# Moving the last chunk of a gated branch's output projection behind the second chunk's state products

## The reference

```python
z, xbc, dt_raw, u, v, ga, gb = split_cols(h @ W['w_in'][l], IN_SIZES)
ya, hs, cs = ssd_branch(z, xbc, dt_raw, conv0[l], ssm0[l], ...)
yb, vr = chunk_mlp_branch(jax.nn.gelu(u), jax.nn.gelu(v), ...)
merged = jax.nn.sigmoid(ga) * (ya @ W['w_ssd_out'][l]) + jax.nn.sigmoid(gb) * (yb @ W['w_cmlp_out'][l])
x = x + g1 * rmsnorm(merged @ W['w_o'][l], W['mix_post_g'][l])
```

```python
def step(h, inp):
    cb = jnp.einsum('btgn,bsgn->btsg', cc, bc)
    mix = cb[..., None] * decay * dtc[:, None]
    y_in = jnp.einsum('btsgr,bsgrp->btgrp', mix, xc)
    y_st = jnp.einsum('btgn,bgrpn->btgrp', cc, h) * jnp.exp(cum)[..., None]
    ...
    h_new = h * jnp.exp(last)[..., None, None] + jnp.einsum('bsgn,bsgr,bsgrp->bgrpn', bc, w_end, xc)
    return h_new, y_in + y_st
```

## Time and profile before

| what | value |
|---|---|
| median of 3 executions | 1935.07 us (1928.68 to 1935.45) |
| the profiled execution | 1933.27 us |
| its span (first to last instruction) | 1931.3 us |
| PE busy | 1759.4 us, 91% of the span |
| mean granted PE clock | 0.945 of full |
| the stage of the change, layer 0 | 284 to 362 us |
| the same stage, layer 1 | 897 to 974 us |

### The profile page before, as it was taken

How to read it: one execution, slowest core, us unless ns; L and a number is a source line. 1 busy time by engine, 2 the same in 40 slices (tenths; PEclk the granted TensorE clock), 3 DMA queues, 4 the chain that set the end, 5 groups by cost and what they waited for, 6 DMA issues and landing times.

```text
span 1931.3 us, 33779 instructions
## 1 busy us (share of the span) xinstructions
PE 1759.4 (91%) x13192; PEld 1633.3 (85%) x13192; DVE 1339.8 (69%) x1664; ACT 1028.1 (53%) x1045; POOL 65.4 (3%) x102
## 2 busy tenths in 40 slices
PE   6999979769999789997795899999999999999995
PEld 4888978758899779997695899989898989899993
DVE  3356776754344546785756688878887889788884
ACT  2344733333333335573332676767676777777771
POOL 4000110000000000020000000000000000000000
PEclk8999998879999989997896899999999999999997
DMA  9797652347886426473230999999999999999980
GB/s 278 251 287 242 204 165 85 101 131 242 280 283 205 144 85 210 133 251 99 66 121 8 344 350 347 355 297 348 346 351 310 330 350 346 338 316 353 344 315 23
DMA packets 379497, 465.06 MB, mean 241 GB/s; under 512 B 10403, under 2 KB 351603, under 8 KB 379378
## 3 DMA queue, kind: packets, MB, share of 16 engines
q1 hardware_dynamic: 372370, 441.65, 69.9%
q0 software_dynamic: 6720, 20.86, 3.5%
q10 hardware_dynamic: 304, 1.08, 0.2%
HBM read 452.84 MB, written 10.92 MB: 240 GB/s over the span
## 4 chain that ended last, share of the span: by engine, by line
PE 80%; DVE 10%; DMA 4%; ACT 4%; issue 2%; POOL 0%; SPq 0%; ACTq 0%; DVEq 0%; POOLq 0%
PE psum L403 9%; PE psum L414 9%; PE psum L408 9%; PE psum L1120 9%; PE psum L1125 9%; PE psum L1122 9%; PE psum L1144 4%; PE psum L1148 4%; PE psum L1145 4%; PE psum L721 2%; PE psum L443 2%; DMA out_ssm_s_dram<-ce 1%; PE psum L1079 1%; PE psum L1096 1%; DMA ce<-in_state_ssm_dram 1%
## 5 line engine op out<-in xcount | busy, mean ns | idle before, releaser
L369 DVE TENSOR_TENSOR wlo<-raw,whi 128x2048 fp32r<-128x2048 f32 x220 | 503.9, 2291 | 113.2 <-ACT whi L364 113.0
L364 ACT ACTIVATE whi<-raw 128x2048 fp32r<-128x2048 f32 x220 | 420.3, 1912 | 35.6 <-PE psum L1148 30.1
L347 DVE TENSOR_TENSOR wlo<-raw,whi 128x2048 fp32r<-128x2048 f32 x112 | 256.7, 2292 | 243.0 <-ACT whi L342 242.5
L403 PE MATMUL psum<-xhi,whi 128*128 128x264 f32 x1584 | 235.2, 303 | 38.9 <-ACT xhi L1206 37.5
L403 PEld LDWEIGHTS psum<-xhi,whi 128*128 128x128 f32 x1584 | 214.2, 201 | 61.3 <-issue 48.1
L342 ACT ACTIVATE whi<-raw 128x2048 fp32r<-128x2048 f32 x112 | 214.9, 1919 | 89.0 <-PE psum L414 64.6
L408 PE MATMUL psum<-xlo,whi 128*128 128x264 f32 x1584 | 214.6, 290 | 0.0
L414 PE MATMUL psum<-xhi,wlo 128*128 128x264 f32 x1584 | 211.2, 286 | 0.0
L408 PEld LDWEIGHTS psum<-xlo,whi 128*128 128x128 f32 x1584 | 205.9, 195 | 0.0
L1120 PE MATMUL psum<-whi,hghi 128*128 128x256 f32 x1408 | 202.2, 286 | 3.0 <-issue 2.1
L414 PEld LDWEIGHTS psum<-xhi,wlo 128*128 128x128 f32 x1584 | 198.0, 188 | 0.1
(11 more groups left out here) (354 smaller groups left out, 1902.8 us busy)
## 6 DMA issues: line engine op xcount, KB each, us to landing
raw<-in_exp_wd_dram SPq DMA_DIRECT2D x76, 1024.0 KB, 5.0
raw<-in_exp_wg_dram SPq DMA_DIRECT2D x72, 1024.0 KB, 6.7
raw<-in_exp_wu_dram SPq DMA_DIRECT2D x72, 1024.0 KB, 6.8
raw<-in_w_in_dram SPq DMA_DIRECT2D x52, 1024.0 KB, 5.4
raw<-in_w_mod_dram SPq DMA_DIRECT2D x17, 1024.0 KB, 5.5
hf<-in_exp_wu_dram SPq DMA_DIRECT2D x16, 1024.0 KB, 6.6
hf<-in_exp_wg_dram SPq DMA_DIRECT2D x16, 1024.0 KB, 6.5
hf<-in_exp_wd_dram SPq DMA_DIRECT2D x12, 1024.0 KB, 4.9
```

Of the source, the lines that this page charges most:

```text
L347: dve.tensor_tensor(wlo[slot], raw[slot], whi[slot].bitcast(F32), ALU.subtract) \
L364: act.activation(whi[j % R3], raw6[slot], ACT.Copy).then_inc(sem["hi_ready"], 1)
L369: dve.tensor_tensor(wlo[j % R3], raw6[slot], whi[j % R3].bitcast(F32), ALU.subtract) \
L403: pe.matmul(out, whi[slot][:, k, j * P:(j + 1) * P], hi(k), start=first and k == 0, stop=False)
```

## The change

In the second scan chunk (c = 1) projection chunk 3 no longer stands between the spread decays and the y products. It is issued behind the loop: on PE behind the state products and ahead of the sums of squares, on DVE behind the folding of the squares and ahead of the update of `hT`. Chunk 1 stays where it was. Nothing is added or taken away, and ACT, POOL and SP keep their order.

```diff
@@ -940,7 +940,8 @@
                     ins.then_inc(sem["cumb_ready"], 1)
-                    cmlp_chunk(2 * c + 1)
+                    if c == 0:
+                        cmlp_chunk(1)
 
                     pe.wait_ge(sem["mix_ready"], v + 1)
@@ -957,6 +958,7 @@
                     ins.then_inc(sem["st_part"], 1)
+                cmlp_chunk(KT // MT - 1)
 
                 for g in range(G):
                     pe.wait_ge(sem["gate_folded"], G * l + g + 1)
```

## The result

The changed kernel takes 1940.66 us (median of 8 runs, 1937.23 to 1944.38), the kernel before 1933.43 us beside it (8 runs). The ratio is 1.0037, 95% interval 1.0024 to 1.0050: 5 to 10 us slower, inside the 0.5% that the prediction took for no change. The forecast was 1939.4.

A forecast was written before the change was run, and what follows sets the result against it. PE bounds most of the kernel, but in this stage DVE and ACT making `mix` do, with chunk 3 free. DVE's 3.2 us plus the y products' 2.9 make 6.1 on 1933.27, so 1939.4 us; range 1932 to 1946.5.

The forecast's parts named there:

- Nothing was won in front of the y products: Ahead of the y products: removing chunk 3's 48 matmuls and DVE's 0.70 us multiplication is worth nothing; `mix` releases them.
- Rival C: Ahead of the y products: chunk 3 was in their way; up to 7.6 us per layer won, 1918; chance 0.03.
- DVE's wait and multiplication: On DVE ahead of `hT`: 0.81 us waiting for chunk 3 plus 0.70 multiplying, 1.6 us per layer, 3.2 for both.
- The y products' clock: Y products after PE's 9.7 us pause: low start, 6.05 us; 0.6 more in layer 0, 2.25 in layer 1, together 2.9.
- Chunk 3 behind the state products at the full clock: On PE behind the state products: chunk 3 takes 5.80 us at full clock, 3.88 of them in an existing pause.
- Rival B: Behind the state products: chunk 3 itself runs at the low clock, +24.5 us, 1958; chance 0.09 including like losses.
- The first products of `ssd_out`: Start of `ssd_out` on PE: low clock as before, no difference counted; bounds 5.15 us less, 2.4 more.
- rival A: From y products through `ssd_out`: work in the pause keeps PE's clock up, giving back up to 5.15 us; chance 0.18.
- The sum: Whole kernel: 3.2 plus 2.9 makes 6.1 us more on the profiled 1933.27 us, giving 1939.4.

The follow-up runs named there:

- e1: Changed kernel with DVE's chunk 3 multiplication moved later, behind the split for `ssd_out`; 1935.85 us, 1.0012 of the kernel before.
- e13: Changed kernel with DVE's multiplication late and chunk 3's 48 matmuls also done, thrown away, ahead of the y products; 1930.97 us, 0.9982 of the kernel before.
- e3: Changed kernel with chunk 3's 48 matmuls also done once, thrown away, at their old place ahead of the y products; 1933.95 us, 1.0003 of the kernel before.
- e2: Kernel before with only DVE's chunk 3 multiplication moved between the folded squares and `hT`, PE unchanged; 1935.53 us, 1.0012 of the kernel before.
- the control: The changed kernel, unaltered, timed once more beside the kernel before; 1938.89 us, 1.0026 of the kernel before.
- e6: Changed kernel with 48 short matmuls added at the program's start, nothing in the stage; 1955.19 us, 1.0123 of the kernel before.
- v4: Kernel before with chunk 2's last two sets moved behind the spread decays and chunk 3's last set behind the state products; 1925.08 us, 0.9968.
- v5: v4 with 30 thrown-away matmuls added ahead of `ssd_out`'s first products; 1921.72 us, 0.9949 of the kernel before.
- v1: Kernel before with chunk 2 moved behind the spread decays, chunk 3 behind the state products, both multiplications late; 1927.79 us, 0.9966.

## Why the prediction was right

*Nothing was won in front of the y products.* Shown: the idle time ahead of them grew from 2.11 to 9.65 us, the releaser is still `mix`, and they start as far behind the spread decays' start as before, 13.48 us against 13.49 in layer 0. Rival C is out.

*DVE's wait and multiplication, 1.6 us per layer.* Shown: 0.84 us of wait (0.81 forecast) and 1.55 in all per layer; taken away, e1 gains 3.0 us, e13 against e3 as well.

*The y products' clock, 0.6 and 2.25 us.* In the profile after 0.91 and 1.88, together 2.79 against 2.85 forecast; over the table's profiles 2.5. The split between the layers was chance, as 5.47 in layer 0 and 3.80 in layer 1 belong to one profile: e2, with the same order on PE, has 3.80 in both. They began at 0.50 in both layers of both profiles of this code. The rule of the Trainium skill that was weighed here ("TensorE: Matmul & The Clock Gate", "Why this matters for your kernels") asked for a low start, and the trace agrees: 0.50 from 323.60 through the pause into the products. The fall itself need not be the pause's work, since in the kernel before the clock also falls right behind the spread decays, with PE busy; but there it is back while chunk 3 runs, and with no chunk there it stays low. The kernel before, during the later part of chunk 3:

```profile
326.00:329.50 3.50, 3.50 (x30) 1.00 0.00 0
```

Filling the pause was worth more than this term, 4.9 us twice. About 1.4 of it belongs to the shorter expert loop of all kernels with added PE work (below); the 3.5 that remain agree with 2.5 to 2.8 within what the intervals allow. What else is in them is not shown.

*Chunk 3 behind the state products at the full clock, 5.80 us.* Shown: 5.82 us, 339.84 to 345.66 in the chain of waits, at 1.00. Rival B is out: the low stretch ended inside the y products.

*The first products of `ssd_out`, counted at 0.* No run shows another value. The profile after alone would say -1.5 us for both layers (9.19 and 9.08 us from the second half of `xhi` to the take-out before, 8.53 and 8.20 after), in the direction of rival A, and the control -0.6. But the table's last column goes from 8.2 to 9.5 in kernels of either order: e2, where chunk 3 stands ahead of the y products, has 8.53 and 8.48, and e1, where it stands behind the state products, 9.17 and 9.01. So this is scatter between profiles, and A's -5.15 is out. e13, 3 us under the kernel before with about 1 of it in the expert loop, would leave room for a small gain from chunk 3's place; no trace shows it.

*The sum.* 6.1 us forecast; 7.2 and 4.8 measured by the medians of the two sets. In the profile after the two terms make 5.9 us (2 x 1.56 and 2.79). The two stages show 3.6 of it, because `ssd_out`'s first products came 1.5 us sooner there and because the kernel before lost 0.75 by chance (its spread decays in layer 1 took longer, 14.24 us to the y products against 13.48). So the mechanism was right, and that the total came so near is in part luck: the profiled loss of 7.8 us has 1.9 at the start of the experts, which the prediction did not name, and some 2 that lie between the two stages in this profile and not in the control's. Whether the change brings about the 1.9 stays open: both profiles of its code have it, e1 and e6 with the same order in the stage on PE do not.

## What to carry to other kernels

Before work is moved off the front of a critical instruction, look at what that instruction waits for: a chunk with idle time behind it is already free, and the one to move is the chunk ahead of the producer of the last wait. Moving it can open a pause, and here the pause was paid in the clock of what came next; leave a piece of the work to hold it (a third of a chunk ahead of the spread decays did, in both layers of v4 and v5). And give a result's consumer the place of its need, not of its producer: DVE's multiplication, with its wait, cost 3 us only because it stood in front of work on the chain.

## What the runs showed of the hardware

PE's clock can fall while PE is busy. In the earlier trace rows it stands at 1.00 while the spread decays run, 4.10 of 4.10 us busy, and at 0.50 right behind them. These matmuls have 16 rows. In v1, where they follow a pause, they ran for 6.5 us at a mean of 0.54.

The expert loop of layer 1, some 750 us long and untouched, runs 1 to 2 us faster in the six kernels that have more PE instructions ahead of it. First and last start of its matmuls on `gthi`, from the view of that tile, in the kernels before, after, e1, e3, e13 and e6:

```profile
L1144 PE MATMUL psum<-whi,gthi x352: 391/394/481, 1145.0 to 1892.5; 128*128 128x512 f32 x176
```

```profile
L1146 PE MATMUL psum<-whi,gthi x352: 391/394/482, 1152.0 to 1899.6; 128*128 128x512 f32 x176
```

```profile
L1146 PE MATMUL psum<-whi,gthi x352: 391/394/481, 1147.1 to 1894.4; 128*128 128x512 f32 x176
```

```profile
L1160 PE MATMUL psum<-whi,gthi x352: 391/394/481, 1146.2 to 1891.9; 128*128 128x512 f32 x176
```

```profile
L1160 PE MATMUL psum<-whi,gthi x352: 391/394/481, 1144.3 to 1890.7; 128*128 128x512 f32 x176
```

```profile
L1148 PE MATMUL psum<-whi,gthi x352: 391/394/481, 1169.2 to 1915.2; 128*128 128x512 f32 x176
```

747.5, 747.6 and 747.3 us without, 745.7, 746.4 and 746.0 with added instructions; the other five without lie at 747.4 to 747.9, the other three with at 746.0 to 746.4. e6, whose stage is that of the changed kernel, says that it is not the stage that does it. The cause was not tried further.

The 96 records of 128x16 matmuls in e6, in fp32 and each with a weight load of 128x128, took 20.66 us, 0.215 each, at a clock of 1.00, though they stream only 16 columns.
